# Level products of the DeltaNet chunk stream: the Z side streams its moving matrix once instead of twice

## The chip, the cores and the metric

The kernel runs on one NeuronCore of a Trainium2 chip. The metric is the device time of one launch in microseconds (us). The kernel before took 3004.05, 3008.09 and 3013.62 us in three timed runs, median 3008.09. TensorE (PE in the profile) runs at one of two clocks, 1.2 or 2.4 GHz; the profile gives the granted share as 0.5 or 1.0.

## The reference

A two-layer encoder over 1040 positions (16 meta tokens and 1024 inputs) of width 1024. Layer 0 is a bidirectional RG-LRU, layer 1 a bidirectional gated DeltaNet with 16 value heads of 128. The change lies in layer 1, in the part that the reference computes chunk by chunk:

```python
a_mat = jnp.where(strict, einsum("bhnid,bhnjd->bhnij", kb, k) * decay, 0.0)
sol = triangular_solve(a_mat + eye, rhs, lower=True, unit_diagonal=True)
u, w = sol[..., :dv], sol[..., dv:]
def step(s, inp):
    v_new = u_n - w_n @ s
    o = qd_n @ s + qk_n @ v_new
    s = s * gt_n + kt_n.T @ v_new
```

Each chunk needs the inverse of a unit triangular matrix (`a_mat + eye`), and a state `s` of 128 x 128 per head and direction runs through the chunks in order.

## The kernel before, in words

The kernel has stages one after another: norms and projections of layer 0, its recurrence, its output projection, norms and projections of layer 1 (`dn_project`), then `dn_chunks`, and last an output projection and the final norm. `dn_chunks` is the stage of the change. It is called the chunk stream below.

Chunks are 104 positions long, ten per sequence (NC = 10). One step g handles one chunk for four systems m = 0..3: two value heads by two directions. There are eight pairs of heads with ten steps each, so 80 steps. A head pair is a stretch of ten steps; two steps (2p and 2p+1) form a period, five periods a pair. Two pairs (STEPS = 20 steps, ten periods) make one turn. After four opening periods come four turns: three are iterations of a hardware loop (`Fori`), the fourth stands behind the loop.

A period has nine slots l = 0..8. Every engine walks through the same slots in program order (`period`, L1673). In slot l each engine first does its share of `inverse(g, l + 1)` for both steps of the period, then prepares (`pre`) for the next period, then does one piece of the state recurrence of the period before, at the slots given in PIECES_AT: piece 0 (L1923) in slots 0 and 5, piece 1 (L1936) in 2 and 6, piece 2 (L1945) in 3 and 7, piece 3 (L1956 and L1957) in 4 and 8. `finish` (L1963) has one product in slots 1 and 6 of the late steps of a pair.

The inverse is found by doubling blocks, in seven levels. A matrix and its transpose are kept side by side: Y products give the next factor, Z products the transposed side. Level 1 (slot 0) multiplies `nhr` and `twos`. Levels 2 to 7 (slots 1 to 6) multiply `old = zz` and `pp`:

- Y: `matmul(bank 2b, stationary zz, moving pp)`, then VectorE masks the result into `pp` (L2065).
- Z: `matmul(bank 2b + 1, stationary pp, moving zz)`, then ScalarE copies the result into `zz` (L1980).

Slot 7 multiplies Y by the unrounded system in plain f32 (L1901), slot 8 makes one last fp32r product with `uu`. A Y or Z group has four products, one per system, in the order m = 3, 2, 1, 0; it is called a quad below. All four results stand side by side in one PSUM bank, 104 columns each.

A quad's products are issued by the helper `widened` (L1860). For m = 3, 2 and 1 it streams the 104-column moving matrix twice, by a broadcast access pattern, into two neighbouring column ranges of the bank (m - 1 and m). The range m - 1 is then overwritten by the next product, since m goes downwards. For m = 0 it streams the matrix once. So a quad takes four weight loads of 104 columns and streams 3 x 208 + 104 = 728 columns. In the profile the doubled products have line L1866 and shape 104x208, the single one L1864 and 104x104. The level products of Y are named `ps<-pp,zz` there (moving first, stationary second), those of Z `ps<-zz,pp`.

The products of the recurrence are in f32. Each such matmul appears as two records with a weight load each (L1923, L1936, L1945, L1956, L1957, L1901, L1963); the shape in a record is that of one pass.

What orders the work around the change is the program order of each engine and its semaphores: the next level of a step waits for `yev` (VectorE's masked copy) and `zev` (ScalarE's copy) of the level before; `ym` and `zm` tell that a quad is done and are raised by its last product (m = 0). In one period of each five (p % 5 == 3) VectorE first copies the tables of the next head pair (`tables`, L2028 to L2035), ahead of its work in slot 0; each iteration of the loop begins with such a period.

Of the kernel before, what the change touches and what calls it, by code (L numbers as in the profile page):

```python
# [34 lines left out]
CH = 104  # L35
# [1572 lines left out]
def dn_chunks(nc, sb, ps, c, tabs, qk_dram, krow_dram, vrow_dram, z_dram, nq_dram, rows_dram, o_dram):  # L1608
# [12 lines left out]
    with Phase(nc) as s:  # L1621
# [34 lines left out]
        def nth(g, i, k):  # L1656

            return g // 2 * 2 * k + 2 * i + g % 2 + 1
# [197 lines left out]
        def _(e):  # L1856
# [3 lines left out]
            def widened(bank, m, lhs, rhs):  # L1860


                if m == 0:
                    return e.matmul(ps[0:CH, bank, 0:CH], lhs, rhs, start=True, stop=True)  # L1864
                o = ps[0:CH, bank, (m - 1) * CH:(m + 1) * CH].rearrange("p (a i) -> p a i", a=2)
                return e.matmul(o, lhs, rhs.unsqueeze(1).to_broadcast([CH, 2, CH]), start=True, stop=True)  # L1866

            def make(n):
                def inverse(g, l):

                    b, q4 = g % 2, g % 4
                    if l == 1:
                        e.wait_ge(nt_done.sem, nt_done.at(n, 2 * g + 1))
                        e.wait_ge(twos_done.sem, twos_done.at(n, g + 1))
                        if g >= 2:
                            e.wait_ge(yev.sem, yev.at(n, nth(g - 2, YS - 1, YS)))
                        for m in MS:
                            ins = widened(2 * b, m, nhr[:, q4, m, :], two(b, m))  # L1880
                        ins.then_inc(ym.sem, 1)
                        if g >= 2:
                            e.wait_ge(tb_done.sem, tb_done.at(n, g - 1))
                        for m in MS:
                            ins = widened(2 * b + 1, m, two(b, m), nhr[:, q4, m, :])
                        ins.then_inc(zm.sem, 1)
                    elif l <= LEVELS:
                        old, p_ = zz[:, b], pp[:, b, (l - 1) % 2]
                        e.wait_ge(yev.sem, yev.at(n, nth(g, l - 2, YS)))
                        e.wait_ge(zev.sem, zev.at(n, nth(g, l - 2, LEVELS)))  # L1890
                        for m in MS:
                            ins = widened(2 * b, m, old[:, m, :], p_[:, m, :])
                        ins.then_inc(ym.sem, 1)
                        for m in MS:
                            ins = widened(2 * b + 1, m, p_[:, m, :], old[:, m, :])
                        ins.then_inc(zm.sem, 1)
                    elif l == LEVELS + 1:
                        e.wait_ge(yev.sem, yev.at(n, nth(g, LEVELS - 1, YS)))
                        e.wait_ge(nt_done.sem, nt_done.at(n, 2 * g + 2))
                        for m in MS:  # L1900
                            ins = e.matmul(ps[0:CH, 2 * b, m * CH:(m + 1) * CH], nq[:, g % NC, m // 2, 0, m % 2, :],  # L1901
                                           pp[:, b, LEVELS % 2, m, :].bitcast(F32), start=True, stop=True)
                        ins.then_inc(ym.sem, 1)
                    else:
                        e.wait_ge(yev.sem, yev.at(n, nth(g, LEVELS, YS)))
                        e.wait_ge(u_done.sem, u_done.at(n, g + 1))
                        for m in MS:
                            ins = widened(2 * b + 1, m, pp[:, b, (LEVELS + 1) % 2, m, :], uu[:, b, m, :])
                        ins.then_inc(zm.sem, 1)
# [50 lines left out]
                def finish(g):  # L1960
# [3 lines left out]
                             start=True, stop=True).then_inc(ssum.sem, 1)  # L1964

                return nothing, inverse, state, finish, nothing

            program(e, nothing, make)
# [181 lines left out]
```

## Time and profile before

| | |
|---|---|
| median of the timed runs | 3008.09 us (3004.05 to 3013.62) |
| profiled execution, own time | 3016.04 us |
| its span (first to last instruction) | 3014.2 us |
| mean granted TensorE clock over the span | 0.936 |
| TensorE matmul busy | 2650.6 us (88%) |
| VectorE busy | 1822.1 us (60%) |
| ScalarE busy | 1228.5 us (41%) |
| GpSimd busy | 1186.7 us (39%) |

Times in the trace are microseconds from the start of the span. The chunk stream lies at about 1750 to 2704 us. Of a matmul the trace gives the start and a duration that contains the way through the array, so neighbouring records overlap; what a product costs TensorE is read from start to start.

### The profile page before, as it was taken

The numbers are of one execution on the slowest core, as the hardware profiler recorded it, in microseconds if no ns is written. First come the engines' busy times: TensorE is split into PE (matmuls) and PEld (weight loads), VectorE is DVE, ScalarE is ACT, GpSimd is POOL, SyncE is SP. The second block draws the span as 40 slices with busy tenths as digits, with TensorE's granted clock in tenths as the row PEclk, the third lists the DMA queues.
The fourth block names the chain that finished last, engine by engine and source line by source line (L and its number), as shares of the span: only waits on it lengthen the run. The fifth ranks groups of instructions, "written<-read, shape, count | busy, mean of one in ns | idle before, by whom it ended". The sixth has DMA issues, their size and how long they took to land. (4 is left out here: it accounts for less than half of the span.)

```text
span 3014.2 us, 52339 instructions
## 1 busy us (share of the span) xinstructions
PE 2650.6 (88%) x18339; PEld 2547.2 (85%) x18339; DVE 1822.1 (60%) x2744; ACT 1228.5 (41%) x2108; POOL 1186.7 (39%) x1111
## 2 busy tenths in 40 slices
PE   4799999984997499999999789998998999995993
PEld 3699999984997399999999789998998999984993
DVE  2266666665302568888888757776776777764004
ACT  2255555564202344444444434553553544543101
POOL 3333333321331234445554345454544555543220
PEclk9899999997998699999999979998998999997996
DMA  3111111112312135555554462424334244214103
GB/s 116 49 36 55 56 56 56 56 42 97 122 42 96 62 81 152 142 148 160 153 155 142 120 160 46 122 46 110 77 82 108 49 110 110 58 32 170 42 28 112
DMA packets 244799, 275.49 MB, mean 91 GB/s; under 512 B 86907, under 2 KB 210380, under 8 KB 242972
## 3 DMA queue, kind: packets, MB, share of 16 engines
q1 hardware_dynamic: 240028, 256.31, 30.4%
q10 hardware_dynamic: 4608, 17.04, 1.4%
q8 instruction: 98, 1.61, 0.2%
q14 instruction: 65, 0.53, 0.1%
HBM read 185.78 MB, written 87.53 MB: 91 GB/s over the span
## 5 line engine op out<-in xcount | busy, mean ns | idle before, releaser
L1980 ACT ACTIVATE zz<-ps 104x416 fp32r<-104x416 f32 x560 | 284.5, 517 | 349.9 <-PE ps L1864 349.9
L595 PE MATMUL ps<-dn_yhi,dn_whi 128*128 128x416 f32 (+1 forms) x1152 | 395.3, 343 | 10.3 <-ACT p_vrow L1486 5.3
L596 PE MATMUL ps<-dn_ylo,dn_whi 128*128 128x416 f32 (+1 forms) x1152 | 376.2, 327 | 0.0
L597 PE MATMUL ps<-dn_yhi,dn_wlo 128*128 128x416 f32 (+1 forms) x1152 | 375.8, 326 | 0.0
L2065 DVE TENSOR_TENSOR pp<-ps,level_mask 104x416 fp32r<-104x416 f32 x480 | 274.8, 587 | 95.4 <-PE ps L1864 93.5
L595 PE MATMUL ps<-rg_yhi,rg_whi 128*128 128x416 f32 (+1 forms) x768 | 257.1, 335 | 57.6 <-POOL rg_wlo L579 37.0
L1866 PE MATMUL ps<-pp,zz 104*104 104x208 f32 x1440 | 269.5, 298 | 28.6 <-DVE pp L2065 20.1
L596 PE MATMUL ps<-rg_ylo,rg_whi 128*128 128x416 f32 (+1 forms) x768 | 256.0, 333 | 0.0
L597 PE MATMUL ps<-rg_yhi,rg_wlo 128*128 128x416 f32 (+1 forms) x768 | 255.1, 332 | 0.0
L1866 PE MATMUL ps<-zz,pp 104*104 104x208 f32 x1440 | 249.8, 284 | 0.0
L595 PEld LDWEIGHTS ps<-dn_yhi,dn_whi 128*128 128x128 f32 x1152 | 218.8, 190 | 17.3 <-issue 15.5
L1866 PEld LDWEIGHTS ps<-pp,zz 104*104 104x104 f32 x1440 | 189.4, 179 | 49.5 <-issue 28.8
L596 PEld LDWEIGHTS ps<-dn_ylo,dn_whi 128*128 128x128 f32 x1152 | 218.8, 190 | 3.5 <-issue 2.5
L597 PEld LDWEIGHTS ps<-dn_yhi,dn_wlo 128*128 128x128 f32 x1152 | 218.7, 190 | 1.2
L1817 POOL TENSOR_TENSOR uu<-zz,ident 104x416 fp32r<-104x416 f32 x80 | 86.4, 1102 | 295.0 <-ACT zz L1980 295.0
L595 PEld LDWEIGHTS ps<-rg_yhi,rg_whi 128*128 128x128 f32 x768 | 150.2, 196 | 60.4 <-POOL rg_wlo L579 37.3
L1866 PEld LDWEIGHTS ps<-zz,pp 104*104 104x104 f32 x1440 | 181.1, 178 | 0.0
L579 POOL TENSOR_TENSOR rg_wlo<-rg_raw,rg_whi 128x1024 fp32r<-128x1024 f32 x48 | 123.3, 2569 | 113.8 <-ACT rg_whi L584 111.2
L595 PE MATMUL ps<-rgo_ohi,rgo_whi 128*128 128x416 f32 (+1 forms) x384 | 126.2, 329 | 43.6 <-POOL rgo_wlo L579 39.5
L577 POOL CAST dn_whi<-dn_raw 128x1024 fp32r<-128x1024 f32 x46 | 63.2, 1374 | 249.8 <-issue 168.4
L595 PE MATMUL ps<-dno_ohi,dno_whi 128*128 128x416 f32 (+1 forms) x384 | 126.4, 329 | 37.9 <-POOL dno_wlo L579 33.8
L897 DVE SCALAR_TENSOR_TENSOR v<-v,xc 128x1040 f32<-128x1040 f32 x32 | 72.8, 2278 | 137.9 <-ACT v L833 137.9
(295 smaller groups left out, 7361.1 us busy)
## 6 DMA issues: line engine op xcount, KB each, us to landing
c_nq<-nq_scratch SPq DMA_DIRECT2D x160, 169.0 KB
dn_raw<-in_dn_w_in SPq DMA_DIRECT2D x48, 512.0 KB, 4.4
qd<-rows_scratch SPq DMA_DIRECT2D x160, 104.0 KB, 3.2
rg_raw<-in_rg_w_in SPq DMA_DIRECT2D x32, 512.0 KB, 4.0
nq_scratch<-p_nq SPq DMA_DIRECT2D x48, 338.0 KB
p_ex<-rows_scratch SPq DMA_DIRECT2D x32, 422.5 KB
nq_scratch<-p_rn SPq DMA_DIRECT2D x32, 338.0 KB
o_scratch<-a SPq DMA_DIRECT2D x16, 520.0 KB
```

Source lines behind the costliest of these rows:

```text
L577: e.tensor_copy(self.hi[:, slot, :], self.raw[:, slot, :]).then_inc(self.hi_done.sem, 1)
L579: e.tensor_tensor(self.lo[:, slot, :], self.raw[:, slot, :], self.hi[:, slot, :], ALU.subtract) \
L595: e.matmul(o, whi, mhi[:, t0:t0 + tn], start=(first and k == 0), stop=False)
L596: e.matmul(o, whi, mlo[:, t0:t0 + tn], start=False, stop=False)
L597: ins = e.matmul(o, wlo, mhi[:, t0:t0 + tn], start=False, stop=(last and k == end))
L897: e.scalar_tensor_tensor(v[:, d, t, :], v[:, d, t, :], 1.0, xc[:, t, :], ALU.add, ALU.mult).then_inc(v_done.sem, 1)
L1817: e.tensor_tensor(uu[:, b, :, :], zz[:, b, :, :].bitcast(F32), eye, ALU.add) \
L1866: return e.matmul(o, lhs, rhs.unsqueeze(1).to_broadcast([CH, 2, CH]), start=True, stop=True)
L1980: e.activation(zz[:, b, :, :], ps[0:CH, 2 * b + 1, 0:m4], ACT.Copy).then_inc(zev.sem, 1)
L2065: e.tensor_tensor(D4(pp[:, b, l % 2, :, :]), D4(Y4), c["level_mask"][:, l, :, 0:CH].unsqueeze(2).to_broadcast([CH, 2, 2, CH]), ALU.mult).t ...
```

## The change

In levels 2 to 7 the Z products no longer go through `widened`. Each of the four streams its moving matrix once into its own 104 columns. The Y products of these levels, both sides of level 1 and the last product with `uu` stay as they are. Results, waits, semaphores, the order of the products and the weight loads are the same.

```diff
@@ -1892,7 +1892,8 @@
                             ins = widened(2 * b, m, old[:, m, :], p_[:, m, :])
                         ins.then_inc(ym.sem, 1)
                         for m in MS:
-                            ins = widened(2 * b + 1, m, p_[:, m, :], old[:, m, :])
+                            ins = e.matmul(ps[0:CH, 2 * b + 1, m * CH:(m + 1) * CH], p_[:, m, :], old[:, m, :],
+                                           start=True, stop=True)
                         ins.then_inc(zm.sem, 1)
```

## Rows read from the trace of the kernel before

**Rows 1.** Windows view of the whole chunk stream, columns in its first line.

```profile
core 0: us, PE busy (x) PEld busy (x) DVE busy (x) ACT busy (x) POOL busy (x), PEclk, DMA share, GB/s
1750.00:2704.30 954.30, 912.11 (x8133) 872.66 (x8132) 680.55 (x1490) 455.63 (x1030) 484.34 (x590) 0.96 0.34 84
```

**Rows 2.** The page's costliest groups: doubled level products, Y then Z.

```profile
L1866 PE MATMUL ps<-pp,zz 104*104 104x208 f32 x1440 | 269.5, 298 | 28.6 <-DVE pp L2065 20.1
L1866 PE MATMUL ps<-zz,pp 104*104 104x208 f32 x1440 | 249.8, 284 | 0.0
```

**Rows 3.** Timeline of TensorE at full clock: start us, duration us, engine, line.

```profile
1840.02 0.49 PE L1866 MATMUL ps<-pp,zz 104*104 104x208 f32 x3
1840.35 0.21 PE L1864 MATMUL ps<-pp,zz 104*104 104x104 f32 x1
1840.40 0.51 PE L1866 MATMUL ps<-zz,pp 104*104 104x208 f32 x3
...
1847.90 0.43 PE L1956 MATMUL ps<-qd,st 128*128 128x104 f32 x2
...
1849.66 0.51 PE L1866 MATMUL ps<-pp,zz 104*104 104x208 f32 x3
...
1855.22 1.63 PE L1901 MATMUL ps<-pp,c_nq 104*104 104x104 f32 x16
1856.69 1.08 PE L1945 MATMUL ps<-vn,kt 104*128 104x128 f32 x8
```

**Rows 4.** Windows view: the five stretches of the stream at half clock.

```profile
1765.80:1775.90 10.10, 10.10 (x59) 10.10 (x58) 4.78 (x8) 3.11 (x6) 7.12 (x9) 0.50 1.02 266
2049.10:2066.00 16.90, 11.25 (x58) 10.36 (x58) 7.64 (x19) 3.73 (x9) 6.26 (x8) 0.50 0.93 261
2291.50:2308.40 16.90, 10.84 (x54) 9.62 (x53) 6.90 (x17) 3.43 (x9) 7.86 (x11) 0.50 0.94 272
2421.20:2431.30 10.10, 10.10 (x56) 10.10 (x56) 4.13 (x10) 3.65 (x9) 5.49 (x7) 0.50 1.00 277
2540.60:2547.30 6.70, 6.53 (x36) 6.53 (x37) 3.38 (x6) 3.01 (x8) 5.93 (x8) 0.50 1.04 313
```

**Rows 5.** Timeline of TensorE around the loop's first back-edge, waits in brackets.

```profile
2045.88 0.53 PE L1866 MATMUL ps<-twos,nhr 104*104 104x208 f32 x3 [1.69 <-issue]
...
2049.94 1.44 PE L1923 MATMUL ps<-st,c_qk 128*104 128x256 f32 x3 [2.06 <-issue]
2056.18 0.85 PE L1866 MATMUL ps<-pp,zz 104*104 104x208 f32 x3 [4.81 <-DVE pp L2065]
...
2061.77 1.99 PE L1936 MATMUL ps<-rr,tb 104*104 104x128 f32 x8
2063.42 0.87 PE L1866 MATMUL ps<-pp,zz 104*104 104x208 f32 x3
...
2066.15 0.21 PE L1864 MATMUL ps<-zz,pp 104*104 104x104 f32 x1
```

**Rows 6.** Timeline of TensorE at the end of the first and of the fourth stretch.

```profile
1774.27 1.92 PE L1936 MATMUL ps<-vrow,tb 104*104 104x128 f32 x8
...
2427.50 2.03 PE L1945 MATMUL ps<-vn,kt 104*128 104x128 f32 x8
2429.18 0.87 PE L1866 MATMUL ps<-pp,zz 104*104 104x208 f32 x3
```

**Rows 7.** Timeline of TensorE: slot 1 of five periods that begin with the tables.

```profile
1816.87 0.53 PE L1866 MATMUL ps<-pp,zz 104*104 104x208 f32 x3 [1.41 <-DVE pp L2065]
...
1932.46 0.54 PE L1866 MATMUL ps<-pp,zz 104*104 104x208 f32 x3 [1.42 <-DVE pp L2065]
...
2175.30 0.54 PE L1866 MATMUL ps<-pp,zz 104*104 104x208 f32 x3 [0.95 <-DVE pp L2065]
...
2418.57 0.54 PE L1866 MATMUL ps<-pp,zz 104*104 104x208 f32 x3 [0.95 <-DVE pp L2065]
...
2538.74 0.54 PE L1866 MATMUL ps<-pp,zz 104*104 104x208 f32 x3 [1.36 <-DVE pp L2065]
```

**Rows 8.** Groups by line, weight loads of Z, at half clock (1765.8:1774.2).

```profile
L1866 PEld LDWEIGHTS ps<-zz,pp 104*104 104x104 f32 x12 | 2.5, 291 | 0.0
```

**Rows 9.** The same view at full clock (1776.3:2044).

```profile
L1866 PEld LDWEIGHTS ps<-zz,pp 104*104 104x104 f32 x420 | 50.0, 170 | 0.0
```

## The prediction

> **What bounds the kernel now.** The change is in the chunk stream only, so I read that stage first: the windows view [rows 1]. TensorE's matmuls are busy 912 of its 954 us, VectorE 681, GpSimd 484, ScalarE 456. TensorE is the bound, and the waits of the others on it cost nothing. What matters is what a product costs TensorE, start to start, and at which clock it runs.
>
> The timeline at full clock gives the first [rows 3]. A quad (four weight loads, 728 streamed columns) takes 0.38 us: 1840.02 to 1840.40. Divided by four that is about 96 ns a product. The single product behind the doubled ones costs no more than they: the next quad starts 0.05 us after it (1840.35, 1840.40), so a once-streamed fp32r product is not slow in itself. The f32 products of slot 7 take (1856.69 - 1855.22) / 16 = 92 ns each, also with 104-column weights and 208 columns in two passes. The sixteen of slot 8 (128-column weights, again 208 columns) take (1849.66 - 1847.90) / 16 = 110 ns. Same streamed columns, more weight columns, 18 ns more: there the weight load sets the pace. For the level products load and stream are near a tie, and that is why streaming the matrix twice costs next to nothing today.
>
> The second is the granted clock. In five stretches of the stream it is 0.50, that is 1.2 GHz, for 10.1 + 16.9 + 16.9 + 10.1 + 6.7 = 61 us [rows 4]; elsewhere it is 2.4. Each of the last four begins at or just behind idle time of TensorE: 1.69, 2.06 and 4.81 us around the first back-edge of the loop [rows 5], the second likewise, 0.95 and 1.36 us in slot 1 of a period that begins with the tables [rows 7]. Three more such idle times (1.41, 1.42 and 0.95 us) did not bring the clock down. What the reader should see is what happens next. In the first stretch TensorE is busy 10.10 of 10.10 us, and in the fourth too, and still the clock stays at 1.2 GHz. Being busy does not lift it. From 2056.18 eight quads run without a gap until 2061.77, at 0.70 us each, and nothing rises; then come the eight products of L1936 until 2063.42, which stream 256 columns per weight load against the quad's 182, and the clock is back within the quads that follow (the product at 2066.15 lasts 0.21 again) [rows 5]. The fourth ends 2.1 us behind L1945, which also streams 256 a load (2427.50 to 2429.18, end 2431.3) [rows 4, 6]. The first ends as an L1936 does (1774.27 and eight times 0.21), and the pattern is the same in all five: four behind an L1936, one behind an L1945. So today the quads alone are not quite enough to bring the clock back, and one group of f32 products among them is.
>
> **The change part by part.** It adds no instruction and no wait. In levels 2 to 7 of 80 steps it makes 80 x 6 x 3 = 1440 Z products [rows 2] stream 104 columns where they streamed 208. A Z quad then streams 416 columns in place of 728.
>
> *At full clock.* The pace falls at most to that of the weight loads. Nothing in the trace streams only 104 columns at length, so I bound it. Lower end: nothing, the loads already set it. Upper end: each product gets shorter by its whole 104 columns, 43 ns at 2.4 GHz, 3 x 43 = 130 ns a quad, 480 quads, 62 us. The nearest row is slot 7: 4 x 92 = 368 ns against some 386 (a mean over neighbouring quads, 0.38 to 0.39), so 18 ns a quad, 480 x 18 = 8.6 us. I take 9 us. That is paid out only while TensorE is the last: the Z copy of ScalarE for a level starts 25 ns sooner, and the other step's two quads still cover it.
>
> The Trainium skill, "TensorE: Matmul & The Clock Gate", section on LDWEIGHTS, puts a weight load at its columns divided by 1.2 GHz. For 104 columns that is 87 ns, a quad at 347 ns and the gain at 19 us, as an estimate by that page; the 92 ns of the nearest row are what I use.
>
> *At half clock.* A Z weight load lasts 291 ns there against 170 [rows 8, 9]: the loads slow down with the clock. So a Z quad at 1.2 GHz still takes about 0.70 us, streaming 43% fewer columns, and there is no gain in these stretches. (Upper bound if the loads did not bind: 3 x 87 = 0.26 us a quad.)
>
> *The clock itself.* This is the term that decides. After the change a slot of levels 2 to 7 has two Y quads as before and two Z quads that leave the array without columns for nearly half of their time. Slots of today already only just bring the clock back, with the help of L1936 or L1945. With thinned Z quads on both sides of it I expect one f32 group to lift it no longer. What is left without a thinned quad is the end of each period: L1936 in slot 6, the sixteen products of L1901 in slot 7, L1945, and the `uu` quads, one behind the other. I expect the clock to come back there, during L1901, once a period, and not before.
>
> How long is that at 1.2 GHz? A slot's four quads take 4 x 0.70 = 2.8 us. The pieces: L1936 1.65 us (2061.77 to 2063.42), L1945 1.68 [rows 5, 6], the sixteen of slot 8 twice their 1.76, so 3.5; L1923, three records in 1.44 us [rows 5], about 1.7 for four. Slots 2 to 6 carry 1.65 + 1.68 + 3.5 + 1.7 + 1.65 = 10.2 us of pieces.
> - After a back-edge TensorE resumes at slot 1: 6 x 2.8 + 10.2 + 2.5 in slot 7 = 29.5 us, where today 9.9 us suffice (2056.18 to 2066.1; the second back-edge has the same pattern and length [rows 4]). 20 us more at half speed cost 10 us. Two back-edges: 20 us.
> - The two falls within a turn's tables period start in slot 2: 5 x 2.8 + 10.2 + 2.5 = 26.7 us against 10.1 and 6.7. Extra 18 each, cost 9 each: 18 us.
> - The three idle times of [rows 7] that the clock withstood lie next to quads that now stream less. I expect two of the three to bring it down, each for 26.7 us: 13 us each, 26 us. (None: 0. All: 40.)
> - The opening stretch (10.1 us today, through slots with few pieces) lasts until slot 7 of its period, about 29 us: 19 / 2 = 9.5 us.
>
> Sum: 20 + 18 + 26 + 9.5 - 9 = +65 us. The trace is of an execution of 3016 us, so it would be 3081 us on its own scale. The timed runs have their median 8 us lower, at 3008, and I carry the difference over: 3073 us.
>
> The other engines get more time beside a slower TensorE, so none of them becomes late; the short waits of 0.3 us for L2065 go away where the clock is low, which is inside the range. Nothing outside the chunk stream changes.
>
> **The rivals.**
> *Idle time alone governs the clock.* Then the change adds no low stretch, and none gets longer; the 9 us of the load-bound quad are all that is left: 2999 us. For it: each fall stands at idle time, and the change adds none. Against it: 10.10 busy microseconds out of 10.10 at 1.2 GHz [rows 4]. The Trainium skill, the same page, its closing table on what matters for kernels, gives just this as its rule: keep TensorE busy and without idle gaps between bursts, and the clock stays. By that rule 2999 would be the answer.
> *The stream sets the pace.* Each product saves its 43 ns and the clock is unchanged: 3008 - 62 = 2946 us. Against it: 92 and 110 ns at the same 208 streamed columns.
> *Half of the clock effect.* One f32 group still lifts the clock, but a quad or two later, and the three idle times stay harmless: five stretches, each some 8 us longer, 5 x 4 - 9 = +11: 3019 us.
> *Hidden both ways.* The 9 us are lost to waits for L2065 and L1980 of the next level, and the clock is as before: 3008 us.
>
> **How the numbers follow.** Main case 0.66, half effect 0.14, idle-only 0.12, stream-bound 0.02, hidden 0.06. A measurement of this kernel can tell about 0.3% (9 us) from no change. Idle-only lies just on that line; I give 0.08 of it to faster and 0.04 to the same. With the stream-bound case faster is 0.10, and with the hidden case and 0.02 of the half effect the same is 0.12; the rest, 0.78, is slower. The range: the main case goes from about 3045 (none of the three idle times counts, 26 us less) to about 3105 (all three, and a return missed here and there, which costs one more period); to hold 8 in 10 it must take in the half effect and touches the idle-only case: 3004 to 3105.
>
> **What would show each step.** In the changed kernel's windows view the stream should have some 180 to 230 us at clock 0.50, in seven or eight stretches of 25 us and more, each ending in L1901 or just behind it. At full clock a Z quad should take 0.36 to 0.37 us, at half clock still about 0.70. The prediction is wrong if the low stretches still end behind L1936 in slots 2 or 3, or if a Z quad at 1.2 GHz takes clearly less than 0.70 us, since then its columns and not its loads were the pace.

## The result and the profile after

The changed kernel takes 3077.53 us, median of four runs (3066.04 to 3089.0), against 3008.35 for the kernel before. The ratio is 1.0227, 95% interval 1.0203 to 1.0251: slower by 69 us. The profiled execution took 3081.76 us with a span of 3079.9, against 3016.04 and 3014.2.

All of it lies in the chunk stream. The windows view of the whole stream, from its first level product to its last product, first before and then after:

```profile
1739.80:2719.60 979.80, 934.67 (x8238) 892.55 (x8238) 687.22 (x1506) 461.06 (x1042) 488.35 (x594) 0.95 0.34 85
```

```profile
1740.50:2785.50 1045.00, 1003.87 (x8238) 959.75 (x8238) 689.64 (x1506) 459.71 (x1042) 485.63 (x594) 0.87 0.32 79
```

The stream grew by 65.2 us and the span by 65.7. The number of matmuls is the same (8238), VectorE, ScalarE and GpSimd are busy as long as before, and TensorE is busy 69 us more. The column before the last two is the granted clock: 0.87 against 0.95.

The stretches at 1.2 GHz, which answer to [rows 4] (the columns are those of [rows 1]):

```profile
1740.50:1790.60 50.10, 49.25 (x270) 48.40 (x271) 21.77 (x40) 14.65 (x31) 18.39 (x21) 0.50 0.78 214
1824.80:1845.30 20.50, 20.16 (x104) 19.62 (x104) 7.79 (x17) 5.79 (x13) 1.19 (x3) 0.50 0.14 17
2060.30:2094.40 34.10, 28.90 (x147) 27.16 (x146) 13.64 (x33) 7.67 (x17) 8.85 (x13) 0.50 0.65 172
2179.70:2193.40 13.70, 13.70 (x71) 13.18 (x71) 6.47 (x15) 4.92 (x12) 7.16 (x9) 0.50 0.10 17
2203.60:2224.10 20.50, 20.31 (x104) 19.80 (x105) 7.69 (x18) 5.69 (x13) 5.35 (x7) 0.50 0.91 234
2326.50:2357.20 30.70, 26.24 (x133) 24.83 (x132) 14.91 (x34) 6.88 (x16) 6.76 (x10) 0.50 0.67 175
2442.60:2456.30 13.70, 13.70 (x72) 13.18 (x71) 6.67 (x14) 4.62 (x12) 7.38 (x9) 0.50 0.09 17
2466.50:2487.00 20.50, 20.50 (x107) 19.98 (x106) 8.59 (x19) 5.42 (x13) 5.20 (x7) 0.50 0.86 235
2572.30:2586.00 13.70, 13.70 (x71) 13.18 (x70) 6.34 (x15) 4.89 (x12) 7.04 (x9) 0.50 0.09 17
2596.20:2616.70 20.50, 20.50 (x108) 19.98 (x106) 8.06 (x19) 5.75 (x13) 5.49 (x7) 0.50 0.83 238
2702.00:2715.70 13.70, 13.70 (x71) 13.18 (x70) 6.37 (x15) 4.88 (x12) 7.15 (x9) 0.50 0.07 16
```

The reader should compare the second and the third number of a row: in nine of the eleven TensorE is busy nearly or fully throughout, and the clock stays low for 13 to 50 us. The opening row begins in both kernels at the stream's start; before the change that part was low for 22.5 us up to 1762.3 and again for the 10.1 us of [rows 4]. The prediction's "elsewhere it is 2.4" overlooks those 22.5 us, and 13.7 us at half clock in the stream's last microseconds (2704.4 to 2718.1); the last microseconds after the change have 13.7 us too, so neither bears on the difference. The ten rows behind the opening hold 191.4 us of busy time at 1.2 GHz; the four of [rows 4] behind its opening hold 38.7.

The last two numbers of a row, the busy share of the DMA engines and their GB/s, settle a rival that [rows 4] suggests, where DMA is at 0.93 to 1.04 in all five stretches: that the transfers hold the clock down. Here five of the eleven stretches have a DMA share of 0.07 to 0.14. And in the kernel before the clock stays at 1.00 beside a DMA share of 1.05, right behind an idle time that it withstood [rows 7]:

```profile
1932.50:1942.50 10.00, 9.72 (x95) 9.59 (x95) 7.76 (x18) 5.11 (x12) 7.72 (x10) 1.00 1.05 312
```

The timeline of TensorE at full clock, which answers to [rows 3] and [rows 7]:

```profile
1823.14 0.53 PE L1866 MATMUL ps<-pp,zz 104*104 104x208 f32 x3 [1.43 <-DVE pp L2066]
1823.51 0.21 PE L1864 MATMUL ps<-pp,zz 104*104 104x104 f32 x1
1823.56 0.53 PE L1895 MATMUL ps<-zz,pp 104*104 104x104 f32 x4
1823.92 0.50 PE L1866 MATMUL ps<-pp,zz 104*104 104x208 f32 x3
```

A quad whose products stream once is called thin. The thin Z quad (L1895) takes 0.36 us, start to start. At half clock, near the end of the second stretch, with the return of the clock at its end:

```profile
1840.37 0.83 PE L1866 MATMUL ps<-pp,zz 104*104 104x208 f32 x3
1840.99 0.29 PE L1864 MATMUL ps<-pp,zz 104*104 104x104 f32 x1
1841.08 0.89 PE L1895 MATMUL ps<-zz,pp 104*104 104x104 f32 x4
1841.78 0.81 PE L1866 MATMUL ps<-pp,zz 104*104 104x208 f32 x3
...
1843.16 1.99 PE L1924 MATMUL ps<-st,c_qk 128*104 128x256 f32 x4
1844.60 0.95 PE L1866 MATMUL ps<-pp,zz 104*104 104x208 f32 x3
1845.38 0.21 PE L1864 MATMUL ps<-pp,zz 104*104 104x104 f32 x1
```

The thin quad takes 0.70 us (1841.08 to 1841.78), as long as the doubled one. The clock returns within the four quads behind L1924 (L1923 in the kernel before), the state product of slot 5. One of its records takes 0.43 us at 1.2 GHz, the time of 512 columns (256 in two passes). Seven of the eleven stretches end so. The other four pass the same product without a return and end in slot 7:

```profile
2189.70 1.99 PE L1937 MATMUL ps<-rr,tb 104*104 104x128 f32 x8
2191.48 2.44 PE L1902 MATMUL ps<-pp,c_nq 104*104 104x104 f32 x15
```

These four begin in slot 4, behind an idle time. Each of the two kernels has seven such waits for ScalarE's copy, of 1.05 to 1.19 us; none of the seven brought the clock down before the change, four do now:

```profile
2175.62 1.12 PE L1946 MATMUL ps<-vn,kt 104*128 104x128 f32 x8
2177.83 0.53 PE L1866 MATMUL ps<-pp,zz 104*104 104x208 f32 x3 [1.09 <-ACT zz L1981]
...
2179.37 0.43 PE L1957 MATMUL ps<-qd,st 128*128 128x104 f32 x2
2179.64 0.53 PE L1958 MATMUL ps<-c_nq,vn 104*128 104x104 f32 x2
2179.96 0.64 PE L1957 MATMUL ps<-qd,st 128*128 128x104 f32 x2
```

From 2179.37 to 2179.96 the duration of two records of slot 4's state products goes from 0.43 to 0.64 us: the clock falls at 2179.7, 1.9 us after the idle time ended, in the midst of work without a gap.

### The profile page after: what moved, and what is told of

Its sections match the earlier page's. It is cut to its first block and busy times, and to the rows that moved or that the text cites. A ratio compares the mean times of both kernels' runs of the same rounds, so it can differ in the third digit from the quotient of the medians.

```text
span 3079.9 us, 52339 instructions
## 1 busy us (share of the span) xinstructions
PE 2720.2 (88%) x18339; PEld 2614.5 (85%) x18339; DVE 1825.5 (59%) x2744; ACT 1227.0 (40%) x2108; POOL 1182.4 (38%) x1111
## 5 line engine op out<-in xcount | busy, mean ns | idle before, releaser
L1866 PE MATMUL ps<-pp,zz 104*104 104x208 f32 x1440 | 289.7, 315 | 28.2 <-DVE pp L2066 19.5
L1895 PE MATMUL ps<-zz,pp 104*104 104x104 f32 x1920 | 288.5, 278 | 0.0
L1866 PEld LDWEIGHTS ps<-pp,zz 104*104 104x104 f32 x1440 | 208.7, 196 | 50.9 <-issue 24.6
L1895 PEld LDWEIGHTS ps<-zz,pp 104*104 104x104 f32 x1920 | 247.4, 195 | 0.0
L595 PEld LDWEIGHTS ps<-dn_yhi,dn_whi 128*128 128x128 f32 x1152 | 218.8, 190 | 17.3 <-issue 15.5
```

The source lines that it names most:

```text
L595: e.matmul(o, whi, mhi[:, t0:t0 + tn], start=(first and k == 0), stop=False)
L1895: ins = e.matmul(ps[0:CH, 2 * b + 1, m * CH:(m + 1) * CH], p_[:, m, :], old[:, m, :], start=True, stop=True)
```

## The experiments

Theory A: the clock falls behind a short idle time and comes back by what TensorE then streams; thin quads stream too little, so the falls become more and the low stretches longer. Rival B: it is the Z side, its chain through ScalarE. Rival C: idle time alone governs the clock. Rival D: thin quads alone let it fall, idle or not.

Times are medians of the timed runs, ratios are against the kernel before, run beside each. The other columns are of the one profiled execution: its own time, which can lie some us beside the median (12 us above it for spread_z_late and both_once, 10 below it for y_once), and "low", the time at 1.2 GHz within the stream. The last column is low without the stream's first 22.5 us and without low stretches in its last 16 us; the expectations count so (61 us before).

| kernel | median us | ratio, 95% interval | profiled, us | low us | as the expectations count |
|---|---|---|---|---|---|
| before | 3008.35 | | 3016.04 | 98 | 61 |
| changed | 3077.53 | 1.0227, 1.0203 to 1.0251 | 3081.76 | 265 | 229 |
| y_once | 3057.08 | 1.0186, 1.0134 to 1.0238 | 3047.2 | 192 | 162 |
| both_once | 3127.68 | 1.0391, 1.0357 to 1.0424 | 3139.78 | 407 | 384 |
| z_third | 3028.91 | 1.0086, 1.0052 to 1.0119 | 3025.36 | 127 | 104 |
| spread_after | 3025.60 | 1.0057, 1.0037 to 1.0076 | 3030.31 | 161 | 135 |
| z_early | 3031.60 | 1.0078, 1.0052 to 1.0103 | 3031.78 | 137 | 111 |
| z_late | 3013.33 | 1.0016, 0.9990 to 1.0042 | 3010.93 | 101 | 72 |
| spread_before | 2989.64 | 0.9924, 0.9901 to 0.9947 | 2989.85 | 72 | 46 |
| spread_before_b | 2989.76 | 0.9944, 0.9925 to 0.9963 | 2983.88 | 52 | 26 |
| spread_z_late | 3003.93 | 0.9988, 0.9975 to 1.0001 | 3016.39 | 134 | 108 |

**y_once: the same columns taken from the other side.**

```diff
-    ins = widened(2 * b, m, old[:, m, :], p_[:, m, :])
+    ins = e.matmul(ps[0:CH, 2 * b, m * CH:(m + 1) * CH], old[:, m, :], p_[:, m, :], start=True, stop=True)
     (Z as in the kernel before)
```

> Mirror of the change: in levels 2 to 7 the Y products stream once and the Z products twice, as many columns taken away as in the change. Theory A (the stream needs its columns to get the clock back, whichever side carries them): low clock stretches of the chunk stream grow from 61 us in all to 180 to 240 us, as in the changed kernel, and the time is 3060 to 3090 us. Rival B (it is the Z side itself, its chain through ScalarE): the time stays within 10 us of 3008. Rival C (idle time alone governs the clock): 2999 us, low stretches 61 us.

Measured: 3057 us, 162 us low as the expectations count. Both are under their bands (3060 and 180 us), so this side costs somewhat less in the runs at hand, though the intervals of the two ratios overlap. It is slower all the same, so rivals B and C fall: columns missing on either side do it.

**both_once: both sides thin.** The edit is the one above on the changed kernel.

> Both sides stream once in levels 2 to 7: twice the columns of the change taken away. Theory A: more and longer low stretches than in the changed kernel, 250 to 310 us, time 3085 to 3120 us; the low stretches end only behind the f32 products of slots 7 and 8, no more behind the one product group of slot 5. Rival C (idle alone): 2990 us, twice the saving of the load-bound quad. A quad at full clock costs 0.36 to 0.37 us on both sides, at half clock 0.70.

Measured: 3128 us, 8 us above the expected band, and 384 us low by the expectations' count, also more than expected. Twice the columns cost some 120 us against 69. Three of its stretches, from its windows view:

```profile
1832.10:1859.20 27.10, 27.10 (x141) 26.58 (x142) 10.69 (x23) 7.54 (x19) 5.52 (x9) 0.50 0.10 11
1934.50:1958.20 23.70, 23.70 (x123) 23.18 (x123) 10.74 (x24) 10.48 (x24) 8.22 (x10) 0.50 0.08 19
2071.10:2094.90 23.80, 23.80 (x123) 23.28 (x123) 10.79 (x24) 10.31 (x23) 8.95 (x10) 0.50 0.06 13
```

These three, and the eleven others, end in or right behind the sixteen products of slot 7, none behind the state product of slot 5: with still thinner quads around it, that one no longer lifts the clock. TensorE is busy 27.10 of 27.10 us at 1.2 GHz, which rival C has no account of.

Nor do all of them begin as theory A has it. The first of the three begins behind an idle time of 1.43 us, but the second and the third, and three of the eleven others (at 2214.3, 2487.4 and 2753.6), have nothing longer than 0.29 to 0.37 us without a matmul in the 12 us ahead of them. For the second:

```profile
1933.19 0.57 PE L1892 MATMUL ps<-pp,zz 104*104 104x104 f32 x4 [0.36 <-DVE pp L2067]
...
1934.33 0.78 PE L1896 MATMUL ps<-zz,pp 104*104 104x104 f32 x4
```

Every fall behind the opening in the kernel before and in the changed one stands behind an idle time of at least 0.88 us. With both sides thin a third of a microsecond is enough.

**z_third: one product in three.**

```diff
+    if m == 3:
+        ins = e.matmul(ps[0:CH, 2 * b + 1, m * CH:(m + 1) * CH], p_[:, m, :], old[:, m, :], start=True, stop=True)
+    else:
         ins = widened(2 * b + 1, m, p_[:, m, :], old[:, m, :])
```

> One of the three doubled Z products of a quad (m = 3) streams once, a third of the change's columns. Theory A: between the two kernels, 3015 to 3045 us, with 80 to 130 us at low clock in the chunk stream. If the effect were all or nothing it would be at 3008 or at 3077; rival C says 3005.

Measured: 3029 us, 127 us low, as expected by A. A third of the columns gives about a third of the loss (22 of 69 us), so the effect is graded. Its profile has four low stretches behind the opening, as many as the kernel before, but of 20 to 31 us instead of 7 to 17: here it is later returns that cost the time, and not more falls.

**spread_after and spread_before: take the idle time away.** The six table copies of VectorE no longer stand in a block ahead of slot 0; one is issued in each of slots 1 to 6 of the same period.

```diff
 for l in range(SLOTS):
     ...
+    if early and 1 <= l <= 6:
+        early(l - 1)          # the table copy number l - 1 of the next pair
 ...
-    if p % PAIRS == 3 and not (last and p > PAIRS):
-        tables(p // PAIRS + 1)
```

> The changed kernel, with the six table copies of VectorE no longer ahead of slot 0 of their period but one each in slots 1 to 6. That takes away the idle time of TensorE in slot 1 (0.95 to 1.86 us at seven places) and adds none. Theory A': an idle time starts each low stretch, the missing columns make it long. Then the stretches that begin in slots 1 and 2 of a tables period go, the idle itself (about 8 us) goes too, and those at the two loop back-edges and the ones behind the wait for ScalarE in slot 4 stay: 110 to 160 us at low clock, 3025 to 3050 us. Rival D (thin quads alone let the clock fall, idle or not): at least 200 us low, 3065 to 3075 us.

Measured: 3026 us, 135 us low by the expectations' count, both as expected by A'. The changed kernel gets 52 us faster once this idle time is gone. Its stretches after the opening:

```profile
2051.20:2085.20 34.00, 31.56 (x160) 30.09 (x159) 13.46 (x36) 9.34 (x22) 11.48 (x16) 0.50 0.65 170
2167.30:2177.40 10.10, 10.10 (x51) 9.58 (x50) 3.76 (x9) 2.94 (x6) 4.25 (x6) 0.50 0.11 23
2300.40:2331.00 30.60, 28.60 (x145) 27.13 (x144) 12.03 (x32) 7.87 (x17) 8.55 (x12) 0.50 0.72 191
2416.40:2430.00 13.60, 13.60 (x70) 13.08 (x69) 6.50 (x14) 4.74 (x12) 7.13 (x9) 0.50 0.09 17
2580.30:2593.80 13.50, 13.50 (x67) 12.98 (x68) 4.86 (x13) 2.62 (x5) 6.23 (x8) 0.50 0.06 17
```

The two long ones are the loop's back-edges; the three others begin behind waits that the edit leaves, two of 1.09 us for ScalarE at slot 4 and one of 2.64 us for GpSimd. The stretches of some 20 us that began in slot 2 are gone. So with one side thin the quads alone do not bring the clock down, and rival D falls for the changed kernel; an idle time of a microsecond next to them does. With both sides thin D is nearly right (both_once above). And thin quads go on costing time beside the idle places that are left: spread_after takes some 36 us more than spread_before, which has the same copies and doubled quads.

> The kernel before with the six table copies spread over slots 1 to 6, as in the run on the changed kernel. The idle time of TensorE in slot 1 goes (7 places, about 8 us, and up to 10 us more at the back-edges), and the falls of the clock that begin in a tables period away from a back-edge (10.2 and 6.8 us low) go with it: 30 to 50 us at low clock, 2985 to 2998 us. If only the idle time matters and the clock stays as it is, 2998 to 3002 us. If the copies cost the same wherever they stand, 3008 us.

Measured: 2989.64 us, ratio 0.9924, 46 us low as the expectations count, and in a second set (spread_before_b) 2989.76 us, ratio 0.9944.

> The spread copies on the kernel before, once more beside it: 2985 to 2994 us.

This version is the fastest of all, 19 us under the kernel before. Its stretches between the opening and the last microseconds are only the two back-edges:

```profile
1738.80:2693.10 954.30, 926.72 (x8238) 887.33 (x8238) 688.17 (x1507) 460.36 (x1042) 488.10 (x594) 0.96 0.34 87
2043.20:2060.10 16.90, 14.94 (x75) 13.98 (x76) 5.87 (x15) 4.76 (x11) 9.59 (x13) 0.50 0.92 251
2282.20:2295.80 13.60, 13.25 (x69) 12.52 (x70) 6.33 (x14) 4.22 (x10) 9.39 (x13) 0.50 0.97 276
```

The stream of this execution is 25.5 us shorter than the one before the change. Less idle time gives more than half of that; most of the rest is time at half clock, above all the two stretches of 10.1 and 6.7 us [rows 4] that are gone. The view of waits of TensorE in the stream, the kernel before and this one (us in total, times, longest):

```profile
PE ps L1866 <- DVE pp L2065: 20.1, 22, 5.0
PE ps L1866 <- ACT zz L1980: 8.5, 13, 1.2
```

```profile
PE ps L1869 <- ACT zz L1983: 8.4, 13, 1.1
PE ps L1869 <- DVE pp L2071: 5.7, 16, 1.4
```

The wait for VectorE fell by 14.4 us, that for ScalarE stayed.

**z_early and z_late: the same number of thin products, in different slots.** The condition in the diff of z_third is `l <= 4` or `l >= 5` for all m instead of `m == 3`.

> The Z products stream once in levels 2 to 4 only (slots 1 to 3), 720 products, half of the change. The low stretches start in slots 0 to 2. Theory A with place: what counts is which slots lie right behind a fall. Here the three slots behind it are thin, so the stretches last until slot 5 or so instead of slot 2 or 3: 120 to 180 us at low clock, 3025 to 3050 us. A theory by count alone (half the columns, half the effect) gives 3040 us here and the same in the late half.

> The other half: the Z products stream once in levels 5 to 7 only (slots 4 to 6), also 720 products. Theory A with place: a stretch that starts in slots 0 to 2 ends in slots 2 or 3 as it does before the change, since nothing is thin there; only an idle time in front of slot 4 could start a new one. 60 to 100 us at low clock, 3000 to 3020 us. By count alone it would be 3040 us, as the early half.

Measured: 3031.6 us for the early half, with 111 us low as the expectations count, under the band of 120 to 180; and 3013.3 us for the late half, with 72 us low, whose interval includes no change. 720 thin products each, and they differ by 18 us. The place counts: thin quads right behind a fall delay the return. The late half is the least steady of all: its ten timed runs go from 2997 to 3028 us, with a mean granted clock of 0.939 in the fastest and 0.931 in the slowest. After the first back-edge the stretch of z_late is 13.50 us long, against 34.10 in the changed kernel:

```profile
2050.70:2064.20 13.50, 8.50 (x42) 7.61 (x42) 7.75 (x17) 2.25 (x5) 7.29 (x10) 0.50 1.00 279
```

**spread_z_late: the spread copies, with thin quads only where I thought them harmless.**

> The table copies spread over slots 1 to 6 and, on top, the Z products of levels 5 to 7 (slots 4 to 6) once. The thin quads then stand only where no fall of the clock lies just in front, except the wait for ScalarE at slot 4. Theory A: the 720 thin products give their full-clock gain, some 5 us (18 ns per quad, 240 quads), against up to two new low stretches at slot 4 (5 us each): 2983 to 2997 us, beside 2990 us for the spread copies alone. If thin quads cost the clock wherever they stand: 3000 us and more.

Measured: 3003.93 us against 2989.76 for the spread copies alone: a miss. The time is 7 us above the band of A; the thin quads cost 14 us instead of giving 5, and what is borne out is the last sentence, 3000 us and more. In the profiled execution, with 3016 us the slowest of the twelve, four of the seven waits for ScalarE at slot 4 brought the clock down. Two of them stand away from the back-edges (1.05 and 1.14 us), and the clock falls 1.9 us after each ended, as in the changed kernel:

```profile
2518.93 0.54 PE L1869 MATMUL ps<-pp,zz 104*104 104x208 f32 x3 [1.05 <-ACT zz L1987]
```

```profile
2520.80:2534.30 13.50, 13.50 (x69) 12.98 (x69) 6.17 (x14) 4.67 (x12) 6.87 (x9) 0.50 0.08 18
2640.30:2653.80 13.50, 13.50 (x69) 12.98 (x69) 6.18 (x14) 4.77 (x12) 6.98 (x9) 0.50 0.07 16
```

I had priced two such stretches at 5 us each; 13.5 us at low clock cost about 6. The rest, in this execution, is an opening that stays low for 55 us where the two profiles of the spread copies have 38 and 24, and the other two falls of slot 4, just ahead of each back-edge (6.8 and 13.7 us low). So the late slots are not harmless: z_late had one fall at slot 4, this kernel four. Which of the seven waits bring the clock down in an execution, and how much the opening differs by itself, the runs do not separate.

## Why the prediction was right

The forecast was 3073 us in a range of 3004 to 3105; measured 3077.53. The sum was +65 us on the profiled execution; it moved by 65.7. Term by term, with the busy time of TensorE at low clock from the windows views. Half speed was priced at one half of that time; I take 0.47, an estimate from the rows: a thin quad takes 0.36 and 0.70 us, a product of slot 4 0.11 and 0.21, and the doubled quad, near its tie at full clock, 0.38 and 0.70, which is 0.46.

| step | predicted | busy low us, before to after | measured |
|---|---|---|---|
| thin quad at full clock | -9 | | some -7 (0.36 against 0.38 to 0.39, about 370 quads) |
| thin quad at half clock | 0 | 0.70 both | 0 |
| two back-edges | +20 | 22.1 to 55.1 | +15.5 |
| two falls of before | +18 | 16.6 to 41.0 | +11.5 |
| two of three held places | +26 | 0 to 40.5 | +19 |
| opening | +9.5 | 31.8 to 49.3 | +8 |
| slot 4, four places | 0 | 0 to 54.8 | +26 |
| sum | +65 | | +73 |

The mechanism held: the loss is time at half clock, 229 us of it in the stream where 180 to 230 were forecast. The steps on the price of a quad held at both clocks, and so did "two of three": the idle places of slot 1 that had been harmless before let the clock fall at 1824.8 and 2203.6, the third did not. The pattern was not the one forecast, seven or eight stretches of 25 us and more that end in slot 7: there are eleven, four of 13.7 us, four of 20.5 and three of 31 to 50.

Two steps were off and made up for each other. First, I had the clock come back only in slot 7. It came back behind the state product of slot 5 in seven stretches, so the slot-2 falls were shorter than forecast (20.5 us and not 26.7). The step that failed is "one f32 group to lift it no longer". What makes the difference between the groups stays open. It is not the columns alone: L1923 with four records of 512 columns and L1936 and L1945 with eight of 256 all stream 2048 columns, and all take about 1.7 us at 1.2 GHz. Nor does L1923 lift the clock by itself: in the four stretches that begin in slot 4 it runs too, and the clock returns only in slot 7. The seven have the groups of slots 2, 3 and 4 ahead of it at half clock, the four only most of that of slot 4; that this is the reason is not shown.

Second, I listed three idle places that the clock withstood and overlooked a fourth kind, the wait of some 1.1 us for ScalarE's copy ahead of slot 4, seven times in the kernel before (one ends at 2158.0). It stands in the same kind of row as those of [rows 7]. Four of the seven let the clock fall, for 13.7 us each, together 26 us. The terms of the forecast that were on its list come to 47 us where they said 65. So that the total fits is luck in part: a term that was missing made up for terms that were too large.

The table's sum is 8 us more than the 65 that the stream grew by. Waits account for some 3 of it (all waits of TensorE in the stream: 37.5 us before, 34.7 after). The remaining 5 us I did not find.

The rivals: idle time alone (2999) and the hidden case (3008) are excluded by the result itself and by y_once, both_once and z_third. The stream-bound case (2946) is excluded by the quad's 0.36 us. The half effect (3019) is excluded by the same rows: two of the three idle places did not stay harmless, and the returns came later by 10 us and more. The rule of the Trainium skill ("TensorE: Matmul & The Clock Gate", section "Why this matters for your kernels") is to keep TensorE busy and to avoid idle gaps between bursts. It is borne out in one half only. Idle time matters, and shorter gaps than those the table warns of: the falls of the two kernels stand behind 0.88 us and more, and taking seven such times away gained 19 us on one kernel and 52 on the other. But being busy did not bring the clock back in 27.10 us (both_once), and with both sides thin the clock fell behind a third of a microsecond.

## What to carry to other kernels

Where small products are bound by their weight loads, streaming the moving matrix twice into columns that are overwritten anyway costs next to nothing at full clock (here 5%, 0.38 against 0.36 us a quad) and keeps the clock up; counting only the work at full clock, one would take it away. Read the granted clock by stretches and look at what ran when it came back. And look for idle times of one microsecond on TensorE even where the engine is 95% busy: moving six small VectorE copies out of one block gained 19 us, and no change to the products gained anything.

## What the runs showed of the hardware that I had not expected

TensorE can be busy without a gap for 27.10 us (both_once) and stay at 1.2 GHz all that time. Taken away evenly over the slots, streamed columns cost by degrees: 480 products (z_third) cost 22 us, 1440 cost 69 (or 50 on the Y side), 2880 cost some 120; 720 products cost 23 or 5 us by their place (z_early, z_late). How short an idle time brings the clock down depends on what is streamed beside it: waits of 1.05 us and more were harmless among doubled quads, four of seven were not beside thin Z quads, and 0.29 to 0.37 us was enough with both sides thin. Weight loads slow down with the granted clock, 170 ns against 291 [rows 8, 9], so a thin quad at 1.2 GHz is no shorter than a doubled one.
